# A two-layer encoder trunk: the steps of the S5 matrices in two halves around a projection block

## What is computed

```python
def _s5_mixer(u, a_re, a_im, b_re, b_im, c_re, c_im, d_skip, log_dt, w_glu):
    ...
    bb_re = cf_re * b_re - cf_im * b_im
    bb_im = cf_re * b_im + cf_im * b_re
    bu_re = jnp.einsum('blgi,gni->blgn', ug, bb_re)
    bu_im = jnp.einsum('blgi,gni->blgn', ug, bb_im)
    ...
    _, _, x_re, x_im = lax.associative_scan(_complex_affine_combine, (..., bu_re, bu_im), axis=1)
    y = jnp.einsum('blgn,gin->blgi', x_re, c_re) - jnp.einsum('blgn,gin->blgi', x_im, c_im)
    y = y.reshape(B, L, S5_WIDTH) + d_skip * u
    ...

for layer in range(DEPTH):
    u = _rmsnorm(h, norm_g[layer])
    (gq, gk, gv, ga, g_gate, s_in, s_gate, aq, ak, av, a_gate, m_gate) = _split_in(u @ w_in[layer])
    ...
    gates = jax.nn.sigmoid(m_gate).reshape(B, L, N_BRANCH, D_MODEL)
    mix = gates[:, :, 0] * y_gla + gates[:, :, 1] * y_s5 + gates[:, :, 2] * y_att
    h = h + mix @ w_out[layer]
```

## Time and profile before

| | |
|---|---|
| device time, 3 runs | median 1890.58 us (1886.93 to 1893.35) |
| span of the profiled execution | 1894.7 us |
| busy: TensorE, its weight loads | 1747.2 us (92%), 1538.7 us (81%) |
| busy: VectorE, GpSimd, ScalarE | 927.3 us, 788.6 us, 701.2 us |
| the chain that ended last: TensorE, of it its blocks (line 844) | 68%, 52% of the span |

### The profile page before, as it was taken

One profiled execution on the slowest core, in us unless ns is written; L12 is line 12 of the kernel. 1 busy time (PEld: TensorE's weight loads), 2 busy tenths in 40 slices (PEclk: granted clock), 3 DMA queues, 4 the chain that ended last, 5 costly groups with the idle time before them and its releaser, 6 DMA issues.

```text
span 1894.7 us, 31165 instructions
## 1 busy us (share of the span) xinstructions
PE 1747.2 (92%) x12985; PEld 1538.7 (81%) x12985; DVE 927.3 (49%) x1471; ACT 701.2 (37%) x1332; POOL 788.6 (42%) x490
## 2 busy tenths in 40 slices
PE   5967899999998999988997999999999898999997
PEld 4967798999887889987897987777788676788885
DVE  7985134333438992374453222533334598624223
ACT  3453442444543113332233543334455322224322
POOL 1655575333232223332343685653332332344442
PEclk8988999999999999998898999999999998999999
DMA  8543244322375653535342433542223956433432
GB/s 146 149 108 105 72 115 118 85 67 72 92 153 131 158 146 107 112 82 149 87 124 55 133 90 90 113 118 78 67 75 101 169 156 155 124 100 92 143 104 85
DMA packets 363539, 209.56 MB, mean 111 GB/s; under 512 B 75524, under 2 KB 350136, under 8 KB 360840
## 3 DMA queue, kind: packets, MB, share of 16 engines
q1 hardware_dynamic: 350600, 187.92, 38.7%
q10 hardware_dynamic: 12800, 19.66, 3.5%
HBM read 170.34 MB, written 36.67 MB: 109 GB/s over the span
## 4 chain that ended last, share of the span: by engine, by line
PE 68%; DVE 10%; POOL 7%; DMA 5%; ACT 5%; issue 3%; SPq 2%; ACTq 1%; DVEq 0%; POOLq 0%
PE ring L844 52%; DMA sb_w_raw<-in_w_in 4%; POOL sb_w_lo L686 3%; PE ring L803 3%; DVE sb_s_prod L1631 2%; PE ring L825 2%; PE aux L1115 1%; SPq L580 1%; PE aux L1224 1%; PE aux L1160 1%; PE aux L1136 1%; DMA s_matrices<-sb_s_phase 1%; DVE sb_s_rot L2136 1%; DVE sb_s_rot L1631 1%; PE aux L1163 1%
## 5 line engine op out<-in xcount | busy, mean ns | idle before, releaser
L686 POOL TENSOR_TENSOR sb_w_lo<-sb_w_raw,sb_w_hi 128x1024 fp32r<-128x1024 f32 x246 | 609.0, 2477 | 1026.3 <-ACT sb_w_hi L1275 1023.9
L1275 ACT ACTIVATE sb_w_hi<-sb_w_raw 128x1024 fp32r<-128x1024 f32 x246 | 260.0, 1057 | 602.7 <-DMA sb_w_raw<-in_w_in 398.7
L844 PE MATMUL ring<-sb_u_hi,sb_w_hi 128*128 128x264 f32 (+1 forms) x2112 | 368.5, 329 | 24.6 <-DVE sb_tmp_dve L1711 14.6
L844 PEld LDWEIGHTS ring<-sb_u_hi,sb_w_hi 128*128 128x128 f32 x2112 | 314.3, 203 | 63.3 <-DVE sb_tmp_dve L1711 16.5
L844 PE MATMUL ring<-sb_u_lo,sb_w_hi 128*128 128x264 f32 (+1 forms) x2112 | 340.8, 312 | 0.0
L844 PE MATMUL ring<-sb_u_hi,sb_w_lo 128*128 128x264 f32 (+1 forms) x2112 | 334.6, 309 | 0.0
L844 PEld LDWEIGHTS ring<-sb_u_lo,sb_w_hi 128*128 128x128 f32 x2112 | 300.6, 192 | 22.0
L844 PEld LDWEIGHTS ring<-sb_u_hi,sb_w_lo 128*128 128x128 f32 x2112 | 294.1, 188 | 21.0
L1307 ACT ACTIVATE sb_tmp_act<-ring 128x528 f32<-128x528 f32 (+1 forms) x112 | 67.3, 601 | 138.6 <-PE ring L844 135.8
L1746 DVE SCALAR_TENSOR_TENSOR sb_tmp_dve<-sb_tmp_act,ring 128x528 f32<-128x528 f32 (+1 forms) x32 | 22.3, 696 | 142.0 <-PE ring L844 130.0
L1551 ACT ACTIVATE sb_att_scores<-sb_att_scores,sb_att_neg_max 128x208 f32<-128x208 f32 x128 | 58.5, 458 | 82.7 <-DVE sb_att_neg_max L1929 82.7
(11 more groups left out here) (333 smaller groups left out, 2455.7 us busy)
## 6 DMA issues: line engine op xcount, KB each, us to landing
sb_w_raw<-in_w_in SPq DMA_DIRECT2D x166, 512.0 KB, 4.1
sb_s_loaded<-s_matrices ACTq DMA_DIRECT2D x16, 1040.0 KB
s_matrices<-sb_s_phase SPq DMA_DIRECT2D x16, 528.0 KB, 3.1
sb_w_raw<-in_w_gla_out SPq DMA_DIRECT2D x16, 512.0 KB, 3.5
sb_w_raw<-in_w_attn_out SPq DMA_DIRECT2D x16, 512.0 KB, 3.5
sb_w_raw<-in_s_w_glu SPq DMA_DIRECT2D x16, 512.0 KB, 3.5
sb_w_raw<-in_w_s_out SPq DMA_DIRECT2D x16, 512.0 KB, 3.5
sb_w_raw<-in_w_out SPq DMA_DIRECT2D x16, 512.0 KB, 3.5
```

Source lines behind the costliest of these rows:

```text
L686: pool.tensor_tensor(WL[:, w], WR[:, w], WH[:, w].bitcast(F32), ALU.subtract).then_inc(lo_ready, 1)
L844: last = pe.matmul(RING[:, 2 * r + hf, 0:c1 - c0], w[:, n % SLOTS, kt, :], moving(b[0], xx[:, kt], c0, c1), start=(term == 0 and kt == 0), ...
L1275: act.activation(WH[:, w], WR[:, w], ACT.Copy).then_inc(hi_ready, 1)
```

## The change

The step is cut in two. TensorE runs the turned inputs (`steps_turned`) ahead of the block that carries the step, through a new `mat_lead`, and the products (`step_products`) behind it. ScalarE makes the first-power copies ahead of the block (`first_powers`), once the products of the step before have been computed, and the other copies behind it. `mbm` and `dsk` get a second buffer, and VectorE waits for the products of step j - 2 in place of j - 1. In `gk`, `gv` and `gq` blocks ScalarE's `mat_turn` moves ahead of the log-sigmoid and the decay exponential.

```diff
-            mbm = sb(f"s5_mb{m}", [P, 2, QUADS, 4, S5_GROUP], at=at_bb)
+            mbm = sb(f"s5_mb{m}", [P, 2, 2, QUADS, 4, S5_GROUP], at=at_bb)
...
-                dsk=sb(f"s5_skip_diag{m}", [P, S5_GROUP], at=at),
+                dsk=sb(f"s5_skip_diag{m}", [P, 2, S5_GROUP], at=at),
...
-            def step_matrices(m, j):
+            def steps_turned(m, j):
 
                 pe.wait_ge(mats_ready, 8 * m + j + 1)
                 h = aux_take(m, ("mbt", j))
...
                 last.then_inc(aux_full[h], 1)
+
+            def step_products(m, j):
+
                 h = aux_take(m, ("toep", j))
                 cam, mb0 = MB[m]["cam"][:, j % 2], MB[m]["mb0"]
                 pe.wait_ge(first_power, 8 * m + j + 1)
...
+            def mat_lead(ly, b):
+
+                if ly == 0 and b in MATS_AFTER and MATS_AFTER[b][1]:
+                    m, k = MATS_AFTER[b]
+                    steps_turned(m, k - 1)
+
             def mat_turn(ly, b):
+
                 if ly or b not in MATS_AFTER:
                     return
                 m, k = MATS_AFTER[b]
                 if k:
-                    step_matrices(m, k - 1)
+                    step_products(m, k - 1)
...
                 for b in BLOCKS[2:17]:
+                    mat_lead(ly, b)
                     project(ly, b, UH, UL)
                     mat_turn(ly, b)
...
                 for j in range(KT):
                     project(ly, ("mg1", j), UH, UL)
+                    mat_lead(ly, ("ws5", j))
...
+                    mat_lead(ly, ("wout", j))
                     project(ly, ("wout", j), MXH, MXL)
                     mat_turn(ly, ("wout", j))
...
-            def matrices_out(m, j):
+            def first_powers(m, j):
 
                 act.wait_ge(mats_ready, 8 * m + j + 1)
+                if j:
+                    aux_result(act, m, ("toep", j - 1))
...
                 last.then_inc(first_power, 1)
+
+            def matrices_out(m, j):
+
                 if j:
                     spilled(act, m, j - 1)
...
+                    mat_lead(ly, b)
                     block_turn(b)
+                    if kind in ("gk", "gv", "gq"):
+                        mat_turn(ly, b)
                     if kind == "ga":
...
-                    mat_turn(ly, b)
+                    if kind in ("sg", "ws5", "wout"):
+                        mat_turn(ly, b)
...
-                if j:
-                    aux_result(dve, m, ("toep", j - 1))
+                if j >= 2:
+                    aux_result(dve, m, ("toep", j - 2))
                 products(BB[:, :, qs], 4, MBM[:, 0], MBM[:, 1], False)
-                link(dve.tensor_scalar(MB[m]["dsk"][:], EYE16[:], SD[:, m, j:j + 1], None, ALU.mult))
+                link(dve.tensor_scalar(MB[m]["dsk"][:, j % 2], EYE16[:], SD[:, m, j:j + 1], None, ALU.mult))
```

More of the change, by code:

```diff
@@ L917, in step_matrices @@
                                   start=(ri == 0), stop=False)
-                last = pe.matmul(AX_[:, 2 * h, 0:S5_GROUP], ID[:], MB[m]["dsk"][:], start=False, stop=True)
+                last = pe.matmul(AX_[:, 2 * h, 0:S5_GROUP], ID[:], MB[m]["dsk"][:, j % 2], start=False, stop=True)
                 if j + 2 < KT:
@@ L1241, in _ @@
                 for j in range(KT):
+                    mat_lead(ly, ("sg", j))
                     project(ly, ("sg", j), UH, UL)
@@ L1250, in _ @@
                     mat_turn(ly, ("ws5", j))
+                mat_lead(ly, ("wout", 0))
                 project_as_made(ly, ("wout", 0), MXH, MXL, mlo_ready, KT * ly)
@@ L1345, in matrices_out @@
                         last = act.activation(MB[m]["mb0"][rows, :, x::2, c0:c0 + S5_GROUP],
-                                              MB[m]["mbm"][rows, :, x::2, 0], ACT.Copy)
+                                              MB[m]["mbm"][rows, j % 2, :, x::2, 0], ACT.Copy)
                 last.then_inc(first_power, 1)
+            def matrices_out(m, j):
                 if j:
@@ L1373, in c_turned, with mat_lead @@
                 last.then_inc(aux_free[h], 1)
+            def mat_lead(ly, b):
+                if ly == 0 and b in MATS_AFTER and MATS_AFTER[b][1]:
+                    m, k = MATS_AFTER[b]
+                    first_powers(m, k - 1)
             def mat_turn(ly, b):
```

6 lines of the change are left out of this document (3 added, 3 removed).

## The result

The changed kernel takes 1903.3 us (median of 20 runs, 1897.7 to 1908.6); the kernel before takes 1892.4 us beside it (median of 20, 1886.9 to 1901.3). The ratio is 1.0053, with a 95% interval of 1.0040 to 1.0066: slower, by 10 to 11 us. The forecast was 1902.

The account below looks back on a forecast made before the run. TensorE, busy 92% of the span, was taken as the bound. First set +15.8 and second set -4.0 us gave +11.8 on the 1890.58 median: forecast 1902 us, its own range some 1890 to 1914, extended down to 1887.

Parts of the forecast that it names:

- The ring: First set: matrices, turned inputs, block, copies, log-sigmoid, exponential, next odd matrices; 27.2 us a turn against 24.2, set +15.8 us.
- First turn: First set, from step 1's matrices ready to step 3's: 28.4 us, including 1.28 for one more table load.
- M(1): First set: moment when step 1's matrices are ready (likewise for other step numbers); left at 101.5 us, off the ring.
- Second turn: First set, from step 3's matrices ready to step 5's: 27.2 us.
- Third turn: First set, from step 5's matrices ready to step 7's: 27.2 us.
- one more hit in a turn: First set: a VectorE instruction lengthened by GpSimd's `w_lo`, 2.2 us a hit; one more in each turn +6.6 us.
- The end: First set, behind step 7's matrices: turned inputs and block gq0 9.1, products 0.6, block gq1 5.8 us, then gq2.
- They buy nothing: First set: two buffers remove VectorE's 10.5 us of waits, but `decay_k` then waits for the exponential, so no gain.
- Second set: Steps on `ws5` and `wout` blocks: some periods longer, `ws5` 3 to 5 -7.7, `ws5` 5 to `wout` 0 -5.6; sum -4.0 us.
- The clock: TensorE restarts at a lower clock after long idling: 2.5 us a place, bounds 1.7 to 3.2, four first-set, three second-set places.
- Hits vanish: Rival, both sets: GpSimd rests while VectorE hurries, saving 19.4 us in all, giving 1883 us; chance 0.09.
- The waits go as meant: Rival: VectorE bound by its work alone, 20.7 us a turn in the first set, giving 1882 us; chance 0.05.

Follow-up runs that it names:

- e2: Changed kernel with the halves kept in the first set alone, second set as before but with two buffers; 1910.6 us, 1.0086 to the kernel before.
- e3: Changed kernel with the log-sigmoids of heads 1 to 3 one block earlier in the first set; 1894.7 us, 0.9988 to the kernel before.
- e10: e3 with VectorE's wait for the spill moved behind a step's first four products; 1891.3 us, 0.9974 to the kernel before.
- e1: Changed kernel with the halves kept in the second set alone, first set as before but with two buffers; 1882.6 us, 0.9934 to the kernel before.
- e6: Kernel before with only the two buffers added; 1887.0 us, 0.9964 to the kernel before.
- e8: e6 with ScalarE's first powers ahead of the block in the second set alone; 1862.8 us, 0.9827 to the kernel before.
- e5: Changed kernel with ScalarE's copies in the first set, except first powers, back behind log-sigmoid and exponential; 1907.2 us, 1.0055 to the kernel before.
- e9: e4 with the early gates of e3 in the first set; 1857.5 us, 0.9810 to the kernel before.
- e11: e9 with VectorE's spill wait behind a step's first four products; 1862.0 us, 0.9831 to the kernel before.
- e4: Changed kernel with TensorE's turned inputs back behind the block, ScalarE's new order and two buffers kept; 1863.1 us, 0.9823 to the kernel before.

## Why the prediction was right, point by point

**The ring, first set: right in its mechanism, and near in its size.** The forecast was +15.8 us, the traces show +12.9 (the change) and +14.8 (e2). e3 and e10 show that it was one of two rings.

- *First turn, 26.1 for 28.4.* The table load and the copies are there. What was missing is the slow clock: the turned inputs of step 1 waited only 1.00 us for M(1), not some 4, and the block ran at full clock (6.62 us from turned inputs to products, at 99.63). The 2.5 us for the clock had no cause here.
- *Second turn, 27.1 for 27.2.* By parts: M(3) to the block's end 8.2 (forecast 9.1), copies 1.8, log-sigmoid and exponential 5.2, VectorE 11.8 (10.9).
- *Third turn, 28.7.* VectorE took 13.3 us instead of 10.9: the four products at 173.33 took 4.57 us where they take 1.70 elsewhere, while GpSimd was at work. The bound for one more hit in a turn, +2.2, nearly covers it. Much of this was there before: the third cycle of before was its longest, 27.9 us, and the mean of 24.2 hid that.
- *The end.* From M(7) to gq2 the forecast had 15.5; it is 15.6, against 9.9 before. So 5.6 us of the loss stand behind M(7), not the "7 to 8" of the prediction: before, block gq1 ran slow behind TensorE's wait (7.7 us from 176.26), and now it runs at full clock.
- *M(1) at 99.5, not 101.5.* I left it where it was. In e1 and e6 to e8, which have the two buffers too but the first-power copies of that set late, it lies at 101.1 to 102.0; in e2 to e5 and e9 to e11, with the copies early, at 98.5 to 99.7. So it goes with ScalarE's order, not with the buffers; by which step, no run shows.

Together: -2.0 for M(1), -2.3, -0.1 and +1.5 for the turns, +0.1 at the end is -2.8, the difference between +15.8 and the trace's +12.9.

**"They buy nothing": right for the change, wrong as a statement on the buffers.** In the ring VectorE waits for the exponential anyway. Alone they bring 0.36% (e6).

**A wait that wasn't forecast.** M(2) came late because VectorE waited 6.14 us for the spill of step 0 (105.66). The text had the spills "come no later". The rows gave the means to see it: the products moved a block away from M, the copy behind them too, and the spill with it. So TensorE waited 3.92 us ahead of gv3, and the wait ahead of gv4, forecast at 9 to 12 us, was only 5.31, since part of it had been waited for already. In the change this costs nothing, as the first ring is longer; in e3 it costs the other half of the gain.

**Waits, listed.** Forecast 50 to 60 us for VectorE's matrices, found 50.3 (with 3.9 of it ahead of gv3, where none was forecast, in place of a longer wait ahead of gv4). Forecast 9 to 12 ahead of gv4, gv6 and gq0: 5.3, 10.0, 11.9. Forecast 4 to 6 ahead of gv1 and gv2: 6.0 and 1.0. No first-power wait: right. 26 to 29 us for the odd gaps: right.

**Second set, -7.3 in the trace for -4.0.** From products to products (856.35, 876.03, 894.44, 913.83, with the waits above) the periods of steps 1 to 3 are 19.7, 18.4 and 19.4 us for the forecast's 19.7 each; `wout` 2 waits 1.35 us for the forecast's 2.0 and `wout` 4 not at all; `ws5` 5 and `wout` 0 don't wait, as forecast. These three are 1.6 us short of the forecast. The term that was most mis-sized is the `wout` pair: 14.8 and 13.2 us for the forecast's 15.2 each, 2.4 us. VectorE's timeline shows a meeting with GpSimd in the one and none in the other (the last two instructions of the input matrices, ready for `wout` 2 and for `wout` 4):

```profile
974.50 2.93 DVE L1662 TENSOR_TENSOR sb_s_mb<-sb_s_mat_prod 128x256 f32<-128x256 f32 x2
...
989.27 0.76 DVE L1662 TENSOR_TENSOR sb_s_mb<-sb_s_mat_prod 128x256 f32<-128x256 f32 x2
```

The forecast had reckoned both from one step of before that held such a meeting. And the forecast took the gain as a thing of the halves; e4 and e8 show that ScalarE's first powers alone bring some 21 to 24 us there, of which TensorE's half gives most back.

**The clock.** The forecast took 2.5 us at each of seven places, from two stretches. The time from the start of the turned inputs to the start of the products is 6.62 us without a wait. Behind the eight waits of 3.4 us and more (gv1, gv3, gv4, gv6, gq0, `ws5` 1 to 3) it is 9.44, 8.15, 7.96, 8.04, 8.94, 9.29, 8.14 and 9.12: a loss of 1.3 to 2.8 us, 2.0 in the mean. One of the seven places, gv2, lost nothing; gv1 and gv3, which the forecast left out, lost 2.8 and 1.5.

**The rivals.** *Hits vanish* (0.09): they didn't. In the first turn the pair at 117.41 takes 2.78 us beside GpSimd's `w_lo` where before it takes 0.9. *The waits go as meant* (0.05): it would need the exponential early; e3 made it so, and still found the spill. The rule of the Trainium skill ("GPSIMD Engine Reference", section "Specifications") that two-input VectorE instructions contend with GpSimd is borne out in kind by these rows; that section gives no price. Here the price is 1.9 to 2.3 us beside `w_lo` (0.88 to 2.78; 1.70 to 4.00 at 127.07), 2.9 beside GpSimd's instructions of 528 columns (173.33), and 0.2 to 0.9 beside its shorter ones (1.93 at 120.11, 2.62 at 146.16).

**How much of the closeness is luck.** The two sets of the change's trace add up to +5.6 us (12.9 - 7.3), half of the forecast's +11.8: the first set was put 2.9 us too long and the second 3.3, and these errors don't cancel. The rest of that trace is 1.6 us shorter than before's. The 20 timed runs show +10.9. Single traces can't settle such a difference: the stretch between the two sets, which no edit touches, is 635.6 to 645.0 us long in the thirteen traces, and the stretch behind the second set 892.8 to 909.7. Part of it may lie in the one trace of before. Its second set takes 155.2 us, that of e2 and of e6, with only the buffers new, 151.4 both. 2.7 of these 3.8 us arise from `ws5` 5 to `wout` 0, and there the difference is TensorE's clock: ahead of `ws5` 5's products it waits 2.74 us in before and 2.80 in e6, and then the first third of the next block takes (before, e6)

```profile
933.08 3.87 PE L844 MATMUL ring<-sb_u_hi,sb_w_hi 128*128 128x264 f32 x16
920.84 2.20 PE L844 MATMUL ring<-sb_u_hi,sb_w_hi 128*128 128x264 f32 x16
```

The granted clock is 0.59 in before (933.0 to 939.0) and 1.00 in e6 (920.0 to 926.0). Were 151.4 us the usual length of before's second set, the two sets would add up to +9.4, near what was measured; if 155.2 is, some 5 us of the agreement with 1902 are luck. With one trace of before this stays open.

## What to carry to other kernels

Work that waits for another engine belongs behind a block that covers the wait; moving it ahead hands the whole wait to the bound engine, and the block with it to every loop that runs through both. Here TensorE's half of the change, the turned inputs ahead of the block, costs 2.3% against the same kernel without it (e4), while the small copies moved ahead on ScalarE, an engine that was only a link, brought 1.4% (e8 against e6). And when one ring is opened, look for the next of nearly its length before counting the gain: follow every consumer of the moved step round to the same buffer, the DMA that spills it too.
